# Means of squares per head as two single-pass products

## The reference, cut to what matters

```python
def head_rmsnorm(o, g):
    of = o.astype(jnp.float32)
    of = of * lax.rsqrt(jnp.mean(of * of, axis=-1, keepdims=True) + RMS_EPS)
    b, s, h, d = o.shape
    return (of.reshape(b, s, h * d) * g.astype(jnp.float32)).astype(o.dtype)
...
        mixed = jnp.concatenate([head_rmsnorm(oa, sb_out_g[l]), head_rmsnorm(ob, ca_out_g[l])], axis=-1)
        x = layer_norm(ALPHA * x + mixed @ w_out[l], ln2_g[l], ln2_b[l])
```

## Time and profile before

| | |
|---|---|
| median of 3 runs | 990.57 us (990.21 to 991.1) |
| the profiled execution, its own time | 991.45 us |
| its span in the trace | 989.7 us |
| mean granted TensorE clock | 0.997 |
| instructions | 17324 |
| busy: PE, DVE, ACT | 98%, 82%, 57% of the span |

### The profile page before, as it was taken

One profiled execution on the slowest core, in us unless ns is written; L12 is line 12 of the kernel. 1 busy time (PEld: TensorE's weight loads), 2 busy tenths in 40 slices (PEclk: granted clock), 3 DMA queues, 4 the chain that ended last, 5 costly groups with the idle time before them and its releaser, 6 DMA issues.

```text
span 989.7 us, 17324 instructions
## 1 busy us (share of the span) xinstructions
PE 971.1 (98%) x6744; PEld 901.7 (91%) x6744; DVE 808.6 (82%) x882; ACT 566.4 (57%) x619; POOL 26.6 (3%) x54
## 2 busy tenths in 40 slices
PE   6999999999999999999999999999999999999996
PEld 6999999899988999999989999998999889999996
DVE  5998887854888998887889988877458889988875
ACT  4655554567875655554565555544787756555543
POOL 2000000001100000000000000000010000000000
PEclk9999999999999999999999999999999999999998
DMA  8656644653334656454626674554624345656441
GB/s 327 209 212 239 243 170 171 213 213 128 128 101 161 212 208 216 169 218 170 244 75 225 212 297 170 212 171 170 213 86 171 132 166 213 219 170 218 171 157 43
DMA packets 33788, 184.14 MB, mean 186 GB/s; under 512 B 3792, under 2 KB 3792, under 8 KB 18640
## 3 DMA queue, kind: packets, MB, share of 16 engines
q1 hardware_dynamic: 32112, 173.55, 49.5%
q0 software_dynamic: 1488, 9.45, 2.5%
q10 hardware_dynamic: 144, 0.52, 0.1%
HBM read 182.46 MB, written 1.05 MB: 185 GB/s over the span
## 4 chain that ended last, share of the span: by engine, by line
PE 87%; DVE 8%; ACT 3%; issue 1%; DMA 1%; POOL 0%; DVEq 0%; SPq 0%; POOLq 0%
PE bank L1167 27%; PE bank L1168 27%; PE bank L1169 27%; PE bank L1296 6%; ACT soft_t L636 1%; DVE w_lo L758 1%; DVE w_lo L764 1%; PE bank L1225 1%; ACT w_hi L430 1%; DVE qT L864 1%; DVE mx L1056 1%; DMA raw<-stream 1%; DVE soft_t L1053 1%; DVE xn L883 1%; DVE xT_lo L825 1%
## 5 line engine op out<-in xcount | busy, mean ns | idle before, releaser
L1167 PE MATMUL bank<-xT_hi,w_hi 128*128 128x256 f32 x1488 | 422.1, 284 | 0.0
L1169 PE MATMUL bank<-xT_hi,w_lo 128*128 128x256 f32 x1488 | 421.0, 283 | 0.0
L1168 PE MATMUL bank<-xT_lo,w_hi 128*128 128x256 f32 x1488 | 421.0, 283 | 0.0
L758 DVE TENSOR_TENSOR w_lo<-raw,w_hi 128x2048 fp32r<-128x2048 f32 x109 | 249.7, 2291 | 74.7 <-ACT w_hi L430 74.3
L430 ACT ACTIVATE w_hi<-raw 128x2048 fp32r<-128x2048 f32 x122 | 232.8, 1911 | 129.7 <-PE bank L1169 128.4
L1168 PEld LDWEIGHTS bank<-xT_lo,w_hi 128*128 128x128 f32 x1488 | 285.3, 192 | 3.0
L1167 PEld LDWEIGHTS bank<-xT_hi,w_hi 128*128 128x128 f32 x1488 | 285.2, 192 | 3.0
L1169 PEld LDWEIGHTS bank<-xT_hi,w_lo 128*128 128x128 f32 x1488 | 285.2, 192 | 0.0
L1167 PE MATMUL bank<-w_hi,h_hi 128*128 128x512 f32 x284 | 111.4, 392 | 0.0
L1168 PE MATMUL bank<-w_lo,h_hi 128*128 128x512 f32 x284 | 111.4, 392 | 0.0
L1169 PE MATMUL bank<-w_hi,h_lo 128*128 128x512 f32 x284 | 110.5, 389 | 0.0
(11 more groups left out here) (153 smaller groups left out, 1228.9 us busy)
## 6 DMA issues: line engine op xcount, KB each, us to landing
raw<-stream SPq DMA_DIRECT2D x110, 1024.0 KB, 4.9
raw<-stream SPq DMA_DIRECT2D x108, 512.0 KB, 4.6
lnp<-ln_gb POOLq DMA_DIRECT2D x6, 1024.0 KB, 5.3
band<-rel_band POOLq DMA_DIRECT2D x2, 1024.0 KB, 9.1
xn<-x POOLq DMA_DIRECT2D x1, 1024.0 KB, 8.2
out<-xn SPq DMA_DIRECT2D x4, 256.0 KB, 2.1
qT<-xT SPq DMA_DIRECT2D x1, 512.0 KB, 4.9
qT<-xT ACTq DMA_DIRECT2D x1, 512.0 KB, 5.0
```

What stands on the lines that cost most here:

```text
L758: nc.vector.tensor_tensor(w_lo[:, at(slot)], raw[:, slot, :], w_hi[:, at(slot)].bitcast(F32), ALU.subtract).then_inc(lo_ready, 1)
L1167: nc.tensor.matmul(o, w[0], x[0], start=start, stop=False, skip_group_check=again)
L1168: nc.tensor.matmul(o, w[0], x[1], start=False, stop=False, skip_group_check=again)
L1169: return nc.tensor.matmul(o, w[1], x[0], start=False, stop=stop, skip_group_check=again)
```

## The change

The float32 product of `head_mean` with the square becomes two fp32r products. ScalarE copies the square, rounded, to `SP_HI[i]`; VectorE subtracts it from the square into `SP_LO[i]`; TensorE multiplies both by a rounded copy of `head_mean` (1/64, the third table of `neg_r`) and adds them in `SS[i]`. TensorE now waits for the subtraction (`sq_lo_done`) and not for the square. On ScalarE each copy stands right behind its square. On VectorE the subtractions of part 0 stand between normalise(3) and w_out_lo(0); those of part 1 stand ahead of and behind mixed_lo(0,1). The one copy that fills `neg_r` grows from 256 to 384 columns.

```diff
-        neg_r = sb("neg_r", [P, 2, P], F32R)
+        neg_r = sb("neg_r", [P, 3, P], F32R)
...
                 nc.scalar.activation(ez[:, i, :], O[part][i][:, :], ACT.Square).then_inc(sq_done, 1)
+                act.wait_ge(sq_done, g + 1)
+                nc.scalar.activation(SP_HI[i], ez[:, i, :], ACT.Copy).then_inc(sq_hi_done, 1)
...
-            nc.scalar.activation(neg_r[:, :, :], table[:, 1:3, :], ACT.Copy).then_inc(neg_ready, 1)
+            nc.scalar.activation(neg_r[:, :, :], table[:, 1:4, :], ACT.Copy).then_inc(neg_ready, 1)
...
+            def square_lo(l, part, i):
+                dve.wait_ge(sq_hi_done, l * 4 + (2 * part + i + 1))
+                nc.vector.tensor_tensor(SP_LO[i], ez[:, i, :], SP_HI[i].bitcast(F32),
+                                        ALU.subtract).then_inc(sq_lo_done, 1)
...
                 normalise(l, 2)
                 normalise(l, 3)
+                square_lo(l, 0, 0)
+                square_lo(l, 0, 1)
                 w_out_lo(l, 0)
                 turned(l, 2)
                 scores(l, 4)
...
                 mixed_lo(l, 0, 0)
                 mix(l, 0, 1)
+                square_lo(l, 1, 0)
                 mixed_lo(l, 0, 1)
+                square_lo(l, 1, 1)
                 w_out_lo(l, 3)
                 mix(l, 1, 0)
                 mix(l, 1, 1)
...
                 for i in range(2):
-                    pe.wait_ge(sq_done, l * 4 + (2 * part + i + 1))
-                    plain(SS[i][:, :], head_mean, ez[:, i, :], start=True, stop=True).then_inc(ss_done, 1)
+                    pe.wait_ge(sq_lo_done, l * 4 + (2 * part + i + 1))
+                    plain(SS[i][:, :], neg_r[:, 2, :], SP_HI[i], start=True)
+                    plain(SS[i][:, :], neg_r[:, 2, :], SP_LO[i], stop=True).then_inc(ss_done, 1)
```

More of the change, by code:

```diff
@@ L256, in trunk @@
         sq_done = sem("sq_done")
+        sq_hi_done = sem("sq_hi_done")
+        sq_lo_done = sem("sq_lo_done")
         ss_done = sem("ss_done")
```

## The result

The changed kernel takes 995.56 us (median of 5 runs, 995.54 to 996.72), the kernel before 990.62 us beside it (990.21 to 991.44). The ratio is 1.005, with a 95% interval of 1.004 to 1.0061: slower by some 4.9 us. The forecast was 995.5 us, inside a range of 992.5 to 997.8.

The account below looks back on a forecast made before the run. The prediction took TensorE and, in the mixer up to ca_turn(5), VectorE's list to bound the kernel. A 2.51 us shift less 0.06 regained, in two layers, gave +4.9 us on 990.57: 995.5 us, range 992.5 to 997.8.

Parts of the forecast that it names:

- What bounds the stage: Mixer, 254 to 286 us in layer 0: VectorE's list bounds it beside TensorE, which has next to no slack.
- the stop: TensorE at ca_turn(5) waits for turned(4), set by VectorE, 0.28 us idle in each layer; gains ahead are worth nothing.
- TensorE's products: head_means: two float32 products of 1.71 us become four single-pass ones of 0.93, saving 0.78 us a pair.
- Part 0: VectorE before w_out_lo(0): 2.51 us later, 1.22 work and 1.29 waiting; the shift arrives whole at ca_turn(5).
- What was put at nothing: ScalarE's copies and later w_out_hi(1) at softmax_exp(4), and the larger neg_r copy at the start: no cost.
- Part 1: head_means(1): TensorE waits for the second subtraction, so of 0.78 us saved only 0.06 us are left.
- A: Whole kernel: TensorE alone decides, so it gets faster, 987.5 us, or 989 if one pair counts; chance 0.05.
- B: VectorE in part 0: only the subtractions' work counts, 1.22 us a layer, giving 992.9 us; chance 0.08.
- D: Whole kernel: shift and gain cancel, no change, 990 to 992 us; chance 0.06.
- C: TensorE after its new pauses: clock falls, some 24 slow products, 2.2 us a layer, giving 1000 us; chance 0.06.

Follow-up runs that it names:

- part 0 alone: Only part 0 gets the copies, subtractions and single-pass products, part 1 keeps its float32 product, against the kernel before: 995.59 us beside 990.88, ratio 1.0048.
- the last run: Changed kernel, subtractions still ahead of w_out_lo(0), with turned(4) first and normalise(5) ahead of the rest of mix(0,0), against the kernel before: 994.17 us beside 990.9.

## Why the forecast was right

**What bounds the stage** was the step that decided. The page put TensorE at 98%, and the chain in order of time put VectorE's list ahead of it from 254 to 286 us. The run with head_means(0) later and the kernel before in another order show both sides of it: 0.78 us a layer saved for nothing, and some 0.5 us a layer won by taking the stop away (0.44 was forecast).

**TensorE's products** take 0.93 us a pair in place of 1.71, as worked out.

**Part 0.** The copies end at the times given (272.01 + 0.63 + 0.81 = 273.45, as forecast). VectorE's pauses are 0.52 and 0.61 us. w_out_lo(0) is late by 2.50 where 2.51 was forecast, and so is ca_turn(5). The split into 1.22 work and 1.29 waiting was argued in the forecast and is shown by the two runs that move the subtractions: of 4.9 us for both layers 2.45 are left, then 0.

**What was put at nothing.** In part 0 ScalarE's copies and the later w_out_hi(1) cost nothing (988.88 us without the subtractions, 995.56 with them). Part 1 has the 0.06 us that were forecast, and alone it changes nothing that can be measured. The larger copy at the start takes 0.51 us (L748), and ScalarE waits 0.41 us for weights behind it, so that it costs nothing either.

**The rivals.** A fell with the run of later means, and B with the change's own time; B's price came out where its condition was made true (2.45 us, where B had 2.3). D didn't occur. C is the one that I had half wrong. I gave the clock's fall 0.06 and priced it at 24 products and 2.2 us a layer. It does fall behind the first pause: in one layer of the profile of the changed kernel, and in both layers of the profiles of part 0 alone and of the last run. What failed in C is the price. The slow products were some 16 a layer, 1.5 us, and I took them as paid in full, but they lie between two pauses and were covered there. Where they aren't covered, they cost about 0.9 us a layer. The forecast had the shift right by its mechanism. That its number held as well was luck as far as the clock goes: an effect that I took for unlikely was likely, and it was free because a pause of 1.6 us, which nobody had chosen for it, stood behind 1.5 us of loss.

## What to carry to other kernels

When an operation is split over three engines, price each part at its place in its engine's list: here the products of a pair saved 0.78 us, and two operations of 0.61 us cost 2.5, since VectorE came to them early, stood 1.3 us for their operands, and everything that the next stop waited for was queued behind them; some positions further on, in idle time that the engine had in any case, they cost nothing. A saving on the busiest engine that lies ahead of a stop which another engine sets is worth nothing; look for `idle before` and its releaser downstream of the saving before you add it up. And when the gain is missing, try the order before giving up the idea.

## What the runs showed of the hardware

TensorE's clock went to 1.2 GHz behind a single idle time of 1.87 or 1.88 us, five times of the six that the profiles of the changed kernel, of part 0 alone and of the last run have. In layer 0 the slow products lasted from 283.1 to 286.4, from 284.5 to 287.9 and from 283.3 to 286.8. It is not certain to fall: behind the same 1.87 us in layer 1 of the changed kernel the granted clock held at 1.00. In the profiles with idle times up to 1.4 us (the subtractions behind w_out_lo(0), and none at all) it stood at 1.00 through both mixers. The Trainium skill (TensorE: Matmul & The Clock Gate, Loop structure matters more than you think) says that TensorE goes cold in a loop with a long wait for a DMA between products. The traces agree in kind, with a single wait for VectorE in place of a DMA, but not each time, as the sixth case shows. What these runs add is that the slow products can be free or not, by what TensorE waits for next.

A float32 product of 512 columns takes 0.855 us, which is 3.7 times the 0.23 of a single-pass product; the two single-pass products that replace it, added up in one bank, take 0.46.
